# Two attentions of a two-block kernel: values stationary, result feature-major, probabilities divided before they are turned

## What is computed

```python
def _softmax_with_sink(logits, sink_b):
    sink_col = jnp.broadcast_to(sink_b, logits.shape[:-1] + (1,))
    return jax.nn.softmax(jnp.concatenate([logits, sink_col], axis=-1), axis=-1)[..., :-1]
...
# first block: q is 256 x 8 heads x 64, keys and values have 2 heads, 256 own + 256 context positions
p = _softmax_with_sink(jnp.concatenate([s_loc, s_ctx], axis=-1), sink_b)
out = p_loc @ v + p_ctx @ v_ctx
...
# second block: 8 heads, 256 latent + 256 context keys, a bias table on the latent part
s = jnp.concatenate([s_loc, s_ctx], axis=-1)
p = jax.nn.softmax(s, axis=-1).astype(v.dtype)
o = p_loc @ v + p_ctx @ v_ctx
```

## Time and profile before

| | |
|---|---|
| median of 3 runs | 1634.06 us (1633.45 to 1634.97) |
| the profiled execution | 1633.81 us |
| its span, first to last instruction | 1632.0 us |
| mean granted TensorE clock | 0.938 |
| busy: TensorE, VectorE, ScalarE, GpSimd | 1324.7, 777.8, 449.0, 325.0 us |
| chain that ended last | PE 42%, DMA 38%, DVE 10%, ACT 5% |
| HBM read | 581.40 MB, 357 GB/s over the span |

### The profile page before, as it was taken

One profiled execution on the slowest core, in us unless ns is written; L12 is line 12 of the kernel. 1 busy time (PEld: TensorE's weight loads), 2 busy tenths in 40 slices (PEclk: granted clock), 3 DMA queues, 4 the chain that ended last, 5 costly groups with the idle time before them and its releaser, 6 DMA issues.

```text
span 1632.0 us, 18887 instructions
## 1 busy us (share of the span) xinstructions
PE 1324.7 (81%) x7044; PEld 759.7 (47%) x7044; DVE 777.8 (48%) x1869; ACT 449.0 (28%) x1223; POOL 325.0 (20%) x272
## 2 busy tenths in 40 slices
PE   5998999999878788779798887699996666667666
PEld 2467886697435454335354542387841221221122
DVE  4101774337787677788888877626420010100001
ACT  2211224313354434454544444224210000000001
POOL 0000000004444444454455444202000000000000
PEclk9999999999989999899999999999997997887888
DMA  9468426928999999999999999954589999999997
GB/s 372 177 255 333 153 104 282 426 94 359 422 421 394 422 418 422 422 405 417 413 417 421 413 422 422 369 206 186 225 361 426 428 426 427 428 427 428 428 428 299
DMA packets 62864, 583.52 MB, mean 358 GB/s; under 512 B 6976, under 2 KB 7360, under 8 KB 9408
## 3 DMA queue, kind: packets, MB, share of 16 engines
q1 hardware_dynamic: 24192, 303.00, 45.0%
q0 software_dynamic: 36864, 268.45, 39.8%
q10 hardware_dynamic: 1728, 11.03, 1.7%
HBM read 581.40 MB, written 1.05 MB: 357 GB/s over the span
## 4 chain that ended last, share of the span: by engine, by line
PE 42%; DMA 38%; DVE 10%; ACT 5%; issue 2%; POOL 1%; SPq 0%; ACTq 0%; PEldq 0%; DVEq 0%
PE ps L1163 39%; DMA slab<-w_stream 18%; DMA big<-peer_uv,big 14%; DVE big L2335 4%; DMA big<-w_stream 4%; DMA scratch<-w_stream 2%; POOL big L735 1%; ACT big L989 1%; PE ps L1433 1%; PE ps L1441 1%; ACT big L985 1%; ACT L981 1%; ACT L976 1%; DVE big L2346 1%; DVE big L2283 1%
## 5 line engine op out<-in xcount | busy, mean ns | idle before, releaser
L1163 PE MATMUL ps<-big 128*128 128x512 f32 (+2 forms) x2054 | 610.7, 556 | 175.7 <-ACT big L989 121.9
L1163 PEld LDWEIGHTS ps<-big 128*128 128x128 f32 (+1 forms) x2054 | 255.6, 176 | 473.0 <-ACT big L989 205.7
L735 POOL DMA_INDIRECT big<-peer_uv,big x256 | 314.0, 1227 | 727.1 <-DVE big L2319 373.4
L2335 DVE CUSTOM_DVE_ANT_0 big<-big 128x1024 f32<-128x1024 f32 x256 | 310.5, 1224 | 118.0 <-DMA big<-peer_uv,big 113.1
L1163 PE MATMUL ps<-xh,slab 128*128 128x128 f32 (+1 forms) x1152 | 172.1, 306 | 1.1 <-ACT xh L785 1.1
L1163 PEld LDWEIGHTS ps<-xh,slab 128*128 128x128 f32 x1152 | 160.3, 193 | 27.2 <-issue 18.2
L1163 PE MATMUL ps<-slab,big 128*32 128x512 f32 x752 | 119.3, 764 | 62.4 <-DMA slab<-w_stream 59.2
L981 ACT ACTIVATE big<-big 128x1 f32<-128x1 f32 x256 | 51.1, 200 | 286.5 <-DVE big L2335 285.8
L2554 DVE TENSOR_TENSOR big<-big,ps 128x512 f32<-128x512 f32 x8 | 5.5, 687 | 226.6 <-PE ps L1163 226.6
L1121 ACT ACTIVATE big<-ps,mod,gain 128x128 f32<-128x128 f32 x32 | 12.1, 457 | 289.3 <-PE ps L1163 289.3
L1163 PE MATMUL ps<-slab,xh 128*128 128x256 f32 (+2 forms) x304 | 88.6, 444 | 3.5 <-ACT xh L785 3.5
(11 more groups left out here) (366 smaller groups left out, 1189.7 us busy)
## 6 DMA issues: line engine op xcount, KB each, us to landing
slab<-w_stream SPq DMA_DIRECT2D x87, 2048.0 KB, 17.7
big<-w_stream SPq DMA_DIRECT2D x35, 2048.0 KB, 32.4
scratch<-w_stream SPq DMA_DIRECT2D x8, 2048.0 KB, 32.3
slab<-w_stream SPq DMA_DIRECT2D x10, 1024.0 KB, 30.2
scratch<-w_stream SPq DMA_DIRECT2D x8, 1024.0 KB, 31.2
big<-w_stream ACTq DMA_DIRECT2D x2, 2048.0 KB, 14.7
big<-peer_uv,big POOLq DMA_INDIRECT x256, 11.4
slab<-w_stream SPq DMA_DIRECT2D x4, 512.0 KB, 17.6
```

The lines of the kernel that those rows point to most:

```text
L735: nc.gpsimd.indirect_dma_start(out=uv[b], out_offset=None, in_=peer_uv, in_offset=bass.IndirectOffsetOnAxis(ap=idxu[:, s:s + 1], axis=0)). ...
L1163: ins = nc.tensor.matmul(*a, **kw)
L2335: V.tensor_tensor_reduce(out=u, in0=u, in1=xtok, scale=1.0, scalar=0.0, op0=ALU.mult, op1=ALU.add, accum_out=dots[:, s:s + 1]).then_inc(do ...
```

## The change

Two heads of one query tile, units 2p and 2p+1, are now handled as pair p (8 pairs per attention):

- The scale 1/8 moves from VectorE's logits to the ScalarE copies that store the queries.
- The score products of both units of a pair go to banks u % 4, and VectorE adds the bias in place in PSUM, reduces the bank, and ScalarE takes the exponential straight from PSUM.
- VectorE divides: a new step `inverse(p)` takes the reciprocal of both sums and multiplies the two `probs` tiles of 128x512 in place, and the transposes wait for that (`shares_ready`).
- `apply(p)` has the values stationary (128x64, one column half of the array per unit) and the turned probabilities moving (128 columns): eight products, alternating between the halves, into bank 5. The result is feature-major and complete; `finish(p)` is one plain 128x128 copy into `aT` or `catT`.
- The turns after each attention, and their ScalarE copies, are gone. All turned probabilities go through the one bank 4.
- SyncE no longer waits for `probsT_filled` before the expert slab SLOTS + 1. The first `out2` products wait for the last pairs one by one. GpSimd's convolution is rewritten into functions with the same order.

```diff
 TensorE
-                def scores(u):
-                    b, h = (u - first) // AH, u % AH
-                    if u >= 2:
-                        pe.wait_ge(scaled, u - 1)
-                    nc.tensor.matmul(bank(u % 2), queries(b, h), keys(h), start=True,
-                                     stop=True).then_inc(scores_filled, 1)
+                def scores(p):
+                    for u in (2 * p, 2 * p + 1):
+                        b, h = (u - first) // AH, u % AH
+                        nc.tensor.matmul(bank(u % 4), queries(b, h), keys(h), start=True,
+                                         stop=True).then_inc(scores_filled, 1)
 
                 def turn_probs(u):
-                    pe.wait_ge(probs_ready, u + 1)
-                    if u >= 2:
-                        pe.wait_ge(probsT_stored, u - 1)
+                    pe.wait_ge(shares_ready, u + 1)
+                    pe.wait_ge(probsT_stored, u)
...
-                def apply(u):
-                    h = u % AH
-                    pe.wait_ge(probsT_stored, u + 1)
-                    if u >= 2:
-                        pe.wait_ge(head_stored, u - 1)
-
-                    chain(bank(4 + u % 2, P), [((probsT2 if blk else probsT1)[u % 3][:, c * P:(c + 1) * P], values(c, h))
-                                               for c in range(4)], head_filled)
+                def apply(p):
+                    pe.wait_ge(probsT_stored, 2 * p + 2)
+                    if p:
+                        pe.wait_ge(head_stored, p)
+                    for c in range(4):
+                        for u in (2 * p, 2 * p + 1):
+                            g = DH * (u % 2)
+                            ins = nc.tensor.matmul(ps[g:g + DH, 5 * 512:5 * 512 + P], values(c, u % AH),
+                                                   probsT[blk][u % 4][:, c * P:(c + 1) * P], start=c == 0, stop=c == 3)
+                    ins.then_inc(head_filled, 1)
...
-                scores(first)
-                scores(first + 1)
+                scores(first // 2)
+                scores(first // 2 + 1)
...
+                for p in range(first // 2, first // 2 + PAIRS):
+                    turn_probs(2 * p)
                     if blk == 0:
-                        if u % 4 == 3:
-                            ada_turn(SETS_MIXED + u // 4, hcT[:, 0:T])
-                        else:
-                            ada_rows(ADA_SETS[SETS_MIXED + u // 4][u % 4])
-                    turn_probs(u)
-                    if u % 2 == 0 and u + 2 < first + UNITS:
-                        pe.wait_ge(scaled, u + 2)
-                        scores(u + 2)
-                        scores(u + 3)
-                    if u > first:
-                        apply(u - 1)
-                    if beside is not None:
-                        beside(u - first)
-                apply(first + UNITS - 1)
+                        ada_beside(2 * p)
+                    else:
+                        for u in (2 * p, 2 * p + 1):
+                            beside(u - first)
+                    turn_probs(2 * p + 1)
+                    if p + 2 < first // 2 + PAIRS:
+                        scores(p + 2)
+                    apply(p)
+                    if blk == 0:
+                        ada_beside(2 * p + 1)
 ScalarE
-                    nc.scalar.activation(probs_of(u), logit_of(u), ACT.Exp, bias=st[:, 0:1],
+                    nc.scalar.activation(probs[blk][u % 4], bank(u % 4), ACT.Exp, bias=st[:, 0:1],
                                          accum_out=st[:, 1:2]).then_inc(probs_ready, 1)
...
                 softmax(first)
+                softmax(first + 1)
...
                 for u in range(first, first + UNITS):
-                    if u + 1 < first + UNITS:
-                        softmax(u + 1)
                     store_turned(u)
+                    if u + 2 < first + UNITS:
+                        softmax(u + 2)
 VectorE
+                        dve.wait_ge(scores_filled, u + 1)
+                        step(V.tensor_tensor(bank(u % 4, T), bank(u % 4, T), bias, ALU.add))
+                        step(V.tensor_reduce(st[:, 3:4], bank(u % 4), X, ALU.max))
...
+                def inverse(p):
+                    sums = stat[:, 8 * p + 1:8 * p + 6:4]
+                    dve.wait_ge(probs_ready, 2 * p + 2)
                     if blk == 0:
+                        dve.wait_ge(sink_ready, 2 * p + 2)
+                        step(V.tensor_tensor(sums, sums, stat[:, 8 * p + 2:8 * p + 7:4], ALU.add))
+                    step(V.reciprocal(sums, sums))
+                    for u in (2 * p, 2 * p + 1):
+                        V.tensor_scalar(probs[blk][u % 4], probs[blk][u % 4], stat[:, 4 * u + 1:4 * u + 2], None,
+                                        ALU.mult).then_inc(shares_ready, 1)
...
                 logits(first)
                 logits(first + 1)
-                for u in range(first, first + UNITS):
-                    if u >= first + 2:
-                        finish(u - 2)
-                    if blk == 0 and u % 4 == 3:
-                        ada(SETS_MIXED + u // 4)
-                    if u + 2 < first + UNITS:
-                        logits(u + 2)
-                finish(first + UNITS - 2)
-                finish(first + UNITS - 1)
+                inverse(first)
+                for p in range(first, first + PAIRS):
+                    if p + 2 < first + PAIRS:
+                        logits(p + 2)
+                    if p + 1 < first + PAIRS:
+                        inverse(p + 1)
+                    finish(p)
+                    if blk == 0 and p % 2:
+                        ada(SETS_MIXED + p // 2)
```

More of the change, by code:

```diff
@@ L31 @@
 UNITS = NT * AH
+PAIRS = UNITS // 2
 RH = 8
@@ L942, in _, with early_out @@
             early = [0]
-            def early_out(dst, o=0, n=512, last=True, shape=None):
+            def early_out(dst, o=0, n=512, last=True, shape=None, scale=1.0):
                 e = early[0]
@@ L1078, in _ @@
             four_out(1, tCS[:, 512:1024])
-            empty(qT2[1])
+            empty(qT2[1], scale=ATT_SCALE)
             four_out(2, foT)
@@ L1083, in _ @@
             attention(1)
-            for n in range(2):
-                turned(8 + n, catT[:, (1 + n) * 512:(2 + n) * 512])
             act.dma_start(final_row, g_final).then_inc(final_loaded, 16)
@@ L1493, in _ @@
             pe.wait_ge(mod_stored, len(ADA_SETS))
-            pe.wait_ge(head_stored, UNITS)
-            for n in range(2):
-                turn(6 + n, [aN[:, t * 512 + j * P:t * 512 + (j + 1) * P]
-                             for j in (2 * n, 2 * n + 1) for t in range(NT)])
             late_branch_m(0)
-            pe.wait_ge(turn_stored, 8)
+            pe.wait_ge(probsT_stored, UNITS)
+            pe.wait_ge(head_stored, PAIRS)
             for j in range(KD):
@@ L1723, in _ @@
             attention(1, last_projection, out2_early)
-            pe.wait_ge(head_stored, 2 * UNITS)
-            for n in range(2):
-                turn(8 + n, [aN2[:, t * 512 + j * P:t * 512 + (j + 1) * P] for j in (2 * n, 2 * n + 1) for t in range(NT)])
-            pe.wait_ge(turn_stored, 10)
             pe.wait_ge(conv_ready, 1)
@@ L1748, in turn_tokens @@
                 for t in range(NT):
-                    turn(10 + 2 * half + t, [xT[:, (4 * half + k) * T + t * P:(4 * half + k) * T + (t + 1) * P]
+                    turn(6 + 2 * half + t, [xT[:, (4 * half + k) * T + t * P:(4 * half + k) * T + (t + 1) * P]
                                              for k in range(4)])
@@ L2230, in attention @@
                 logits(first)
                 logits(first + 1)
-                for u in range(first, first + UNITS):
-                    if u >= first + 2:
-                        finish(u - 2)
-                    if blk == 0 and u % 4 == 3:
-                        ada(SETS_MIXED + u // 4)
-                    if u + 2 < first + UNITS:
-                        logits(u + 2)
-                finish(first + UNITS - 2)
-                finish(first + UNITS - 1)
-            attention(0, aN)
+                inverse(first)
```

145 lines of the change are left out of this document (68 added, 77 removed).

## The result

| | before | changed |
|---|---|---|
| median, us (4 runs each) | 1634.19 (1633.45 to 1634.97) | 1656.46 (1654.94 to 1660.60) |
| ratio | | 1.0136, 95% interval 1.0124 to 1.0149 |
| profiled execution, span, us | 1633.81, 1632.0 | 1657.21, 1655.4 |
| mean granted clock of TensorE | 0.938 | 0.929 |

The change costs 22.3 us, 1.4%. The forecast was 1647.5 in a range of 1639 to 1655: right in sign, 9 us too small in size, and the range missed by 1.5.

What follows compares the result with a forecast made beforehand. TensorE was taken to bound the second attention and, nearly full, to share the first with DMA's slabs. 1633.8 + 6.7 + 2.4 + 4.5 = 1647.4, the median 0.25 higher: 1647.5 us, range 1639 to 1655.

Steps and rivals of the forecast that it cites:

- The loop: Both attentions: scores, logits, first share, transposes and next scores wait in turn through VectorE; second attention 6.13 us per pair against 4.79.
- Rival 4: Both attentions: the loop does not close, TensorE stays the bound at 3.82 a pair; kernel at 1623.5; chance 0.06.
- The `apply` of 1.7 to 2.0: Both attentions: `apply` takes this many us if its 16 loads are slow and unhidden; sum some 2 us higher.
- The clock, +4.5: Both attentions: TensorE's idle gaps lower its granted clock, three falls at 1.5 us each.
- The bound of 10: Upper bound of the clock term, 10 us: a fall in nearly every second pair of the attentions.
- rival 1: Both attentions: the loop through VectorE, with falls of the clock; kernel at 1644 to 1653; chance 0.6.
- Second attention, +6.7: From first scores to `out2`: 51.3 us against 44.6, through the loop, with the turns' gain in it; bounds +6.2 to +9.4.
- First attention, +3.3 without the turns: First attention: the loop at 7.57 us per pair and a slab wait of 2.1 end it at 321.0 against 317.7.
- the turns alone give -0.9: After the first attention: the turns that the change removes had taken 0.87 us there.
- Rival 3: Both attentions: the loop with long shares, slow `apply` and ten microseconds of clock; 1653 to 1660; chance 0.1.
- long shares: Both attentions: a share takes 0.69 us instead of 0.48; +3 us over both.
- slow `apply`: Both attentions: an `apply` of 1.7 us instead of 1.0, put at +2 us in the costly case.

Runs made afterwards that it cites:

- f2: The changed kernel with shares ahead of the logits on VectorE and the exponential ahead of the copy on ScalarE; 1639.42 us, ratio 1.0031.
- h: f2 with the first slab's products ahead of all scores, scores and `apply` between the transposes, shares between the logits; 1631.36 us, ratio 0.9982.
- busy4: The changed kernel with throwaway TensorE products during waits for shares, nine ahead of the first pair, then four; 1650.13 us, ratio 1.0094.
- seq: The changed kernel with the products of the two column halves one unit after the other instead of alternating; 1657.30 us, ratio 1.0143.
- late: The changed kernel with GpSimd's convolution also waiting for the first two shares of the second attention; 1650.41 us, one run.
- noconv: The changed kernel with GpSimd's convolution replaced by its last product alone; 1656.73 us, one run.

## Why the prediction missed

**The sign and the mechanism held.** The loop closed through VectorE as worked out: 6.41 per pair in the second attention (forecast 6.13), 7.77 in the first (7.57), TensorE idle about 2 us ahead of the transposes, ended by the shares (0.48 for one, as forecast), `apply` at 1.09 (1.0), everything from `out2` on at its old length. The clock's price of 1.5 us a fall held as well. Rival 4 (the loop does not close) fell for this program order; f2 and h show what it would have been, a second attention of 42.7 and 39.4 where rival 4 had 44.6 - 7.8 - 1.6 = 35.2. The `apply` of 1.7 to 2.0, worked out from a row under the rule of the Trainium skill on the mode change (TensorEngine Tiling (Array Packing), Key Properties and the list of feature incompatibilities), did not come: at 1.09 the trace speaks against a charge of that size here. It does not speak against the rule itself.

**What failed was the size, in four terms.** The largest are the clock, three falls where five came, and the second attention, where GpSimd beside the shares stood at nothing and a period was 0.28 short.

1. **The clock, +4.5.** "I take three" falls "at 1.5". There were five in the attentions of the profiled execution, and busy4 measures 7.5 us. The price was right, the count was off, and no row stood behind it. The length of a gap alone does not give the count: every gap of 2.03 in the first attention took the clock down, and of the seven of 2.10 to 2.47 in the second, one. In the other kernels that keep these gaps, it was again all four long ones of the first (seq, late, noconv; in seq three of them were only 1.54 long), and one or two of the second. Why it is so in the first is open. The bound of 10 was in the text, but my range for rival 1 stopped at 1653. Short 3.0.
2. **Second attention, +6.7.** Without the clock (busy4) it was 54.4 against my 51.3 from the first scores to `out2`. Of the 3.1, 1.2 (0.96 and 0.2) is GpSimd beside the shares, which I did not price though the earlier trace rows list 3.63 us of GpSimd in the stretch; 1.4 is five periods that are each 0.28 longer, nearly all of it transposes and side products, 1.99 instead of the 1.76 that I put together from groups of before; 0.5 lies in the start and the end.
3. **First attention, +3.3 without the turns.** busy4 gives +4.0: short 0.7. The wait for a slab was 1.07 at full clock, where I had 2.1, and a period was 0.2 longer.
4. **Outside the change.** In the profiled pair, 1.7 us ahead of the first attention and 1.5 between the attentions (+0.6 where the turns alone give -0.9). The 1.7 goes with a fall of the clock at 138.8 that lasted longer than before's, in code that the change does not touch; the other kernels here that leave that code alone began their first scores between 253.80 and 256.53. The 1.5 lies within the 786.6 to 790.0 us that the same code between the attentions took. So both are taken for scatter of the profiled executions, of which there is one each, and not for an effect of the change. The medians are 22.3 apart and not 23.4; of their distance to the forecast, 9.0, the first three terms name 6.8, and the other 2 stay open.

3.0 + 3.1 + 0.7 + 3.2 - 0.3 = 9.7, of the 9.8 between the forecast's 13.6 and the 23.4 found.

**The range.** Rival 3 (costly ends, 1653 to 1660) is where the result lies, though not by its long shares and slow `apply`, neither of which came: that the result fell into it is in part luck. I gave it 0.1, and my upper end, 1655, takes in only its lower edge. Two things should have widened it: a fall behind every long gap of the first attention, and GpSimd beside the shares. That the gaps and GpSimd's work would be there was to be had from rows; what they cost was not.

## What to carry over

When a step is put on an engine between "wait for X" and "feed X", look at what that engine's queue holds ahead of it: here two lines of VectorE's order were worth 16 of the 22 us. A saving on an engine that idles is worth little until the loop is opened (the alternation: nothing that the intervals can tell, and then 6.9 us). Price a new gap on TensorE twice: its length, and the products behind it at half speed (1.5 us a fall here, behind 5 of 11 long gaps); and when a step moves behind a wait, ask which ring slot it frees.

## What was not expected of the hardware

- A share of 128x512 from SBUF to SBUF took 0.48 us alone and 1.46 when a GpSimd product of two SBUF tiles (1.26 us) had started 0.08 before it; the biases and reductions on PSUM beside the same convolution kept their 0.42 and 0.69. The Trainium skill, SBUF — State Buffer, Who interferes with whom, has it that the two engines have a port pair in common that one holds for a whole instruction, a `tensor_scalar` in a two-port mode included. The trace agrees roughly: by an estimate from its rows, 1.26 - 0.08 of waiting and a share of 0.40 to 0.48 would be 1.58 to 1.66, against 1.46. Which mode the share ran in, no run here shows.
- Alternating column halves saves 0.49 of 1.58 us for 16 records, not half of it.
- A gap of 2.03 us took the clock down each time in the first attention, and one of 2.26 most times not in the second.
- A reduction over 512 columns takes 0.69 from PSUM, as from SBUF before.
